# Opening of a two-block transformer kernel: the turns of the input moved around the first weight products

## The reference, cut to what matters

```python
c_act = jax.nn.silu(c)
mod = (c_act @ ada_w[0] + ada_b[0])
shift, scale, gate = jnp.split(mod, 3, axis=-1)
h = rmsnorm(x, norm_g[0]) * (1.0 + scale) + shift
proj = h @ ret_w_in            # 2048 x 12288, float32
```

## Time and profile before

| | |
|---|---|
| median of three runs | 2283.14 us (2281.1 to 2284.38) |
| profiled execution, its own time | 2281.51 us |
| its span | 2279.8 us |
| TensorE busy | 2221.4 us, 97% |
| weight loads into TensorE busy | 1844.3 us, 81% |
| DVE busy | 1488.4 us, 65% |
| ACT busy | 1038.5 us, 46% |
| mean DMA rate | 220 GB/s |

### The profile page before, as it was taken

One profiled execution on the slowest core, in us unless ns is written; L12 is line 12 of the kernel. 1 busy time (PEld: TensorE's weight loads), 2 busy tenths in 40 slices (PEclk: granted clock), 3 DMA queues, 4 the chain that ended last, 5 costly groups with the idle time before them and its releaser, 6 DMA issues.

```text
span 2279.8 us, 27033 instructions
## 1 busy us (share of the span) xinstructions
PE 2221.4 (97%) x10412; PEld 1844.3 (81%) x10412; DVE 1488.4 (65%) x1903; ACT 1038.5 (46%) x1353; POOL 98.9 (4%) x81
## 2 busy tenths in 40 slices
PE   5999999999999999999989999999999999999999
PEld 4878788878887788988868788877888888888887
DVE  7898778778877878556665555655555554555554
ACT  4544354444444445545454455444444344344442
POOL 0000000000000000000020200000100000000000
PEclk8999999999999999999989999999999999999999
DMA  9988577877896779545435554564666666666664
GB/s 349 379 330 291 170 269 270 308 263 286 297 312 214 293 252 330 184 132 174 167 128 205 154 175 142 168 194 152 189 185 186 194 186 192 193 185 193 187 188 143
DMA packets 139795, 501.92 MB, mean 220 GB/s; under 512 B 15633, under 2 KB 16145, under 8 KB 139153
## 3 DMA queue, kind: packets, MB, share of 16 engines
q1 hardware_dynamic: 139376, 499.99, 66.3%
q10 hardware_dynamic: 290, 0.21, 0.0%
HBM read 498.04 MB, written 2.10 MB: 219 GB/s over the span
## 4 chain that ended last, share of the span: by engine, by line
PE 88%; DVE 5%; DMA 3%; ACT 2%; issue 2%; POOL 1%; SPq 0%; DVEq 0%; ACTq 0%; POOLq 0%
PE ps L996 71%; PE ps L1007 7%; PE ps L1068 2%; PE ps L1021 2%; DMA raw<-in_ret_in 1%; PE ps L1060 1%; DVE wlo L1549 1%; DVE raw L1556 1%; DMA arena<-in_ret_in 1%; ACT whi L1241 1%; PE ps L1159 0%; POOL arena L1951 0%; DVE alo L1549 0%; PE ps L1136 0%; PE ps L1137 0%
## 5 line engine op out<-in xcount | busy, mean ns | idle before, releaser
L1549 DVE TENSOR_TENSOR wlo<-raw,whi 128x1024 fp32r<-128x1024 f32 (+1 forms) x711 | 864.4, 1221 | 585.4 <-ACT whi L1241 582.4
L1241 ACT ACTIVATE whi<-raw 128x1024 fp32r<-128x1024 f32 (+1 forms) x711 | 739.5, 1044 | 807.2 <-PE ps L996 651.9
L996 PE MATMUL ps<-whi,ahi 128*128 128x512 f32 x2482 | 788.0, 397 | 7.0 <-ACT whi L1241 4.0
L996 PE MATMUL ps<-wlo,ahi 128*128 128x512 f32 x2482 | 771.1, 390 | 4.8 <-DVE wlo L1549 4.7
L996 PE MATMUL ps<-whi,alo 128*128 128x512 f32 x2482 | 771.1, 391 | 0.0
L996 PEld LDWEIGHTS ps<-wlo,ahi 128*128 128x128 f32 x2482 | 466.1, 188 | 106.3 <-DVE wlo L1549 7.7
L996 PEld LDWEIGHTS ps<-whi,alo 128*128 128x128 f32 x2482 | 466.7, 188 | 98.4
L996 PEld LDWEIGHTS ps<-whi,ahi 128*128 128x128 f32 x2482 | 456.6, 189 | 99.6 <-ACT whi L1241 4.1
L1556 DVE SCALAR_TENSOR_TENSOR raw<-raw,arena 128x1024 f32<-128x1024 f32 x184 | 223.9, 1219 | 0.2
L1007 PE MATMUL ps<-whi,ahi 128*128 128x512 f32 x254 | 99.6, 392 | 0.0
L1007 PE MATMUL ps<-wlo,ahi 128*128 128x512 f32 x254 | 98.9, 389 | 0.0
(11 more groups left out here) (207 smaller groups left out, 1371.8 us busy)
## 6 DMA issues: line engine op xcount, KB each, us to landing
raw<-in_mlp SPq DMA_DIRECT2D x256, 512.0 KB, 4.2
raw<-in_ret_in SPq DMA_DIRECT2D x188, 512.0 KB, 5.0
raw<-in_ada_t SPq DMA_DIRECT2D x184, 512.0 KB, 5.0
raw<-in_in SPq DMA_DIRECT2D x80, 512.0 KB, 4.3
raw<-in_ret_out SPq DMA_DIRECT2D x64, 512.0 KB, 4.9
raw<-in_mla_in SPq DMA_DIRECT2D x48, 512.0 KB, 4.6
raw<-in_mla_out SPq DMA_DIRECT2D x32, 512.0 KB, 3.7
raw<-in_out SPq DMA_DIRECT2D x32, 512.0 KB, 4.1
```

The source lines that it names most:

```text
L996: mm = e.matmul(acc_[:, :], (ahi, alo, ahi)[m][:, slot, kb, tb * P:(tb + 1) * P], parts[m][:, chunk(n)], start=first and m == 0, stop=False)
L1241: e.activation(high(i)[:, 0:ncol], raw_of(n)[:, 0:ncol], ACT.Copy).then_inc(*s_hi.up(i))
L1549: e.tensor_tensor(low(i)[:, 0:ncol], raw_of(n)[:, 0:ncol], high(i)[:, 0:ncol].bitcast(F32), ALU.subtract).then_inc(*s_lo.up(i))
```

## The change

Five edits, all in the opening:

1. `pump(0, 3)` becomes `pump(0, 1)`: only load 0 and its adt stand before `norm_diag` in the list, where three did.
2. The DVE operation that makes the mean of h0 moves from `norm_diag` into `opening`, right behind the sums.
3. w0 is taken without a call of `pump`, so loads 6 to 23, their adt, mods and the splits of w2 to w7 no longer stand before block w0 but are queued by `next_block` for w1, together with loads 24 to 26 and the split of w8.
4. Behind block w0 come the turns of pairs 2 to 5 alone, in four banks that are free by then; the xn_out of each stands before those splits now.
5. The turns of pairs 6 and 7 become side jobs behind phase 0's side-by-side part: they run after blocks w8 and w9.

It follows that mod_first of kb 1 stands behind block w1 (and behind the split of w8), where it stood before block w1.

```diff
-    pump(0, 3)
+    pump(0, 1)
     do("norm_diag", "h0")
     pump(0, 6)
     turn_first(0)
...
-                w = next_block()
+                if kb == 0 and name == names[0]:
+                    w = at["used"]
+                    at["used"] += 1
+                else:
+                    w = next_block()
                 if i < len(kbs) - 1:
                     do("block", 0, ("h0", kb), w, 1024, got[name], begin)
-                    if kbs[0] == 0 and i == 0 and name == names[0]:
-                        for k2 in range(2, 8):
+                    if kb == 0 and name == names[0]:
+                        for k2 in range(2, 6):
                             turn_first(k2)
...
         if ph == 0:
+            side += [lambda k2=k2: turn_first(k2) for k2 in (6, 7)]
             do("later_in")
...
                 e.tensor_reduce(stat[:, 8:10], stat[:, 0:4].rearrange("p (t c) -> p t c", t=2), AX_X, ALU.add).then_inc(*s_vec.up(("sums", "h0")))
+                w.wait_ge(*s_vec.on(("sums", "h0")))
+                mean("h0", 0)
...
+            def mean(src, o):
+                e.tensor_scalar(stat[:, o + 10:o + 12], stat[:, o + 8:o + 10], 1.0 / D, EPS, ALU.mult, ALU.add).then_inc(*s_vec.up(("mean", src)))
+
             def norm_diag(src):
                 o = SUMS[src]
                 if src != "h0":
                     mean_square(src, o)
-                w.wait_ge(*s_vec.on(("sums", src)))
-                e.tensor_scalar(stat[:, o + 10:o + 12], stat[:, o + 8:o + 10], 1.0 / D, EPS, ALU.mult, ALU.add).then_inc(*s_vec.up(("mean", src)))
+                    w.wait_ge(*s_vec.on(("sums", src)))
+                    mean(src, o)
                 w.wait_ge(*s_pool.on(("rstd", src)))
```

## The result

The changed kernel takes 2288.16 us (median of nine runs, 2286.08 to 2289.53) against 2281.93 (nine runs, 2281.1 to 2284.38) before. The medians lie 6.2 us apart, the means 5.3; the ratio, which agrees with the means, is 1.0023 with a 95% interval of 1.0013 to 1.0034. The forecast was 2286.8, which is +3.7 us on the 2283.14 of the first three runs, and the range 2281.4 to 2289.4. The profiled span is 2286.4 us.

The account below looks back on a forecast made before the run. TensorE, busy 97% of the span, was taken as the bound, setting the pace from w2. 0.65 + 1.0 + 1.9 + 1.87 - 1.74 = +3.7 us on 2283.14 gave 2286.8 us, range 2281.4 to 2289.4.

Parts of the forecast that it names:

- likeliest case: Opening: w2 0.65 + L later, slow clock there, two turns added, wait at w32 gone: +3.7 us, 2286.8; chance 0.52.
- persistent wait: Rival at w32: later restart of loads carries through and the 1.74 us come back: +5.4, 2288.6; chance 0.12.
- upper clock bound: At w2: highest cost taken for TensorE's slow stretch after the long wait, 2.2 us against 1.9 forecast.
- first rival: At w0: block wholly slow, L = 2.0 instead of 1.0, w2 stretch at its 2.2: +5.0, 2288.1; chance 0.22.
- clock at w2: At w2: TensorE idles before it and meets it at 1.2 GHz, costing 1.9 us, bounds 1.5 and 2.2.
- L: At w0: cost of running at low clock after a gap behind the first turns; taken as 1.0 us, upper bound 1.9 to 2.2.
- The early turns: Opening: turns of pairs 0 and 1 start about 3.3 us earlier, near 13.1 instead of 16.42.
- The chain on DVE: From w2's rest to w7's: copies ahead of w2's split delay DVE, w7's rest ends 46.3 + L, w2 starts 0.65 + L later.
- The two turns: After w8 and w9: turns of pairs 6 and 7 move into TensorE's gapless part, costing 1.87 us.
- What is given back: At w32: TensorE arrives 1.87 us later than the loads do, so a wait of 1.74 us goes.
- two faster cases: At w2: delay hidden, start 47.8, -1.6 us, chance 0.08; or w2 5.35 early, -5.2 us, 2277.9, chance 0.06.
- hidden delay: On DVE: copies of pairs 2 to 5 cost splits nothing, w2 starts at 47.8; best end -1.6, 2281.5; chance 0.08.

Follow-up runs that it names:

- first and second experiments: First: changed kernel, mean and diagonals behind three adt again, ratio 1.0017. Second: kernel before with only the mean and diagonals moved early, ratio 1.0000.
- four blocks ahead: Staged kernel with its list running only four weight blocks ahead of the products up to w31, mean and diagonals behind three adt: ratio 0.9972, median 2275.70 us.
- third experiment: Changed kernel with splits of w2 and w3 queued before block w0, ahead of the four copies, mod_first of kb 1 behind w1: ratio 1.0004.
- filled wait: Changed kernel with 84 more matmuls in front of block w1, adding nothing to the output: ratio 1.0016.
- six turns: Changed kernel with the turns of pairs 6 and 7 also behind w0, their copies ahead of the split of w2: ratio 1.0025.
- two splits first: Same run as the third experiment: splits of w2 and w3 ahead of the four copies in the changed kernel, ratio 1.0004.
- late mean: Mean and diagonals behind three adt again (edits 1 and 2 undone); in the changed kernel ratio 1.0017, also combined with other runs.
- staged order: Changed kernel, list to w3's split before w0, w5's before w1, w7's before w2: ratio 1.0001; with mean and diagonals behind three adt 0.9994.

## Why the prediction was right, and where it was off

**Direction and size.** Forecast +3.7 us as the likeliest, measured +5.3 by the means and within the range. The forecast's own narrower range, up to 2288.1, was just missed by the median, 2288.16. Of the chances, "the same" within 0.2% had 0.62 and "slower" 0.32; the ratio says 0.23% slower, with an interval (0.13 to 0.34%) that holds both. By the prediction's own signs its likeliest case did not come: it called itself wrong if w2 started after 53, and w2 started at 53.25; w7's rest was to end by 48.3 and ended at 48.73. The upper edge of the range, 2289.4, does not follow from its terms either: the persistent wait with the upper clock bound gives 2283.14 + 5.4 + 0.3 = 2288.8. The case that came in kind was the first rival, w0 wholly slow, at +5.0. That its number lies so near the 5.4 of the rows is part luck: it had the clock at w2 0.45 too high, and left out 0.5 at w0 and 0.5 at w8's load.

**L, the clock at w0.** This is the term that was mis-sized: the sum has L = 1.0, the middle between two bounds, of which it said that neither is shown. The rows give 2.53, above the upper bound of 2.2. Of that 2.33 is twelve matmuls of which nearly all ran at half pace, 0.2 the later start of w0. The first and second experiments show that the early mean did this and that it costs only where the copies hold DVE; w0 was slow in all eight profiles with the early mean and in one of five with the late. What in it did so stays open: the turns began earlier and a gap of 3.1 us lay behind them, but four blocks ahead had a slow w0 behind a gap of 0.55. The Trainium skill, "TensorE: Matmul & The Clock Gate", section "HAM oscillation — how this bites in real kernels", describes such a pattern, a short piece of matmuls, a gap and the next piece at the low clock. The trace agrees in kind, since the twelve matmuls after the gap ran at 1.2 GHz (0.85 us a pair); the 4.8 us behind the gap of 0.55 are not told by it.

**The early turns.** The prediction had them at 13.1; they began at 14.04, since POOL's operation between the mean and the diagonals took 1.62 us and not 0.72. The gap was 3.1 us instead of 3.8.

**The chain on DVE.** Right, and shown by the third experiment: with L = 2.5 the prediction gives w7's rest at 48.8 and load 24 at 42.5; the rows have 48.73 and 42.47. Missing was 0.5 us: I had w8's load in time, at 49.0, and it landed at 50.55, 6.6 us after its issue at 43.98 behind two others, not 3.6 plus 1.3 each. From 44.5 to 50.5 the DMA moved 336 GB/s, where the prediction had 405. w2 came 3.70 late: 0.65 + 2.53 + 0.5.

**The clock at w2.** 1.9 us forecast, 1.75 measured, and shown by the filled wait.

**The two turns.** 1.87 forecast, 1.80 measured.

**What is given back.** 1.74 forecast; 3.70 + 1.75 + 1.80 - 5.38 leaves 1.87. The size is right, the reason only in part. The prediction let the loads move with w2 and put just the two turns between them and TensorE. In the rows TensorE reaches w8 5.46 us later, but the last split before w32's banks ran only 3.63 later (134.71 against 131.08), and DVE's wait for mod_first of kb 4 and 5, the tie that the prediction names, ended only 3.38 later (73.97 against 70.59). ACT's copies of finished banks, behind which it stands, came 3.4 later (70.25 against 66.83): before, they had themselves stood behind splits that waited for loads. The 1.8 us by which the loads moved less take the wait away with or without the turns, as reckoned at the six turns. In the two splits first the loads moved by 0.46 (131.54), and there the turns do carry it: w32 at 133.52 found banks whose copies began at 132.51.

**The other rivals.** The persistent wait and the two faster cases did not come. The third experiment built the hidden delay on purpose, and its shift of +0.4 is near the -1.6 that I gave as its best end plus the 1.75 of clock that I had left out there.

## What to carry to other kernels

On an engine that works strictly in order, what counts is not that a copy is early but what stands behind it and in front of it: a copy that must wait for TensorE delays the splits behind it (here 5 us), and a copy behind a split that waits for a far load delays TensorE (here 16, 1.5 and 10.7 us). Look for that pattern before moving work between engines, and limit how far loads are queued ahead where banks must be freed: here, with the late mean in both, that took the ratio of the staged order from 0.9994 to 0.9972. Work done earlier in front of a wait that stays can also be paid for in clock: 2.3 us at w0 behind the early turns, 1.75 at w2 behind the long wait. And before a term is put at the middle of two bounds, ask what either end would change; here L alone decided between +2.7 and +4.7.

## What the runs showed of the hardware that was not expected

The granted clock in the profile reads 1.00 in the first 30 us of the changed kernel, also while matmuls run at half pace (0.85 us a pair at 21 us, as under 0.50 at 53 us). There only the pace of the matmuls tells the level.

The rows show when the clock rose, not why. With the early mean w0 was slow in all eight profiles: 4.2 to 5.3 us from its start to the next turn. With the late mean it took 2.9 us in four of five profiles, and 4.8 in the fifth (four ahead), behind the same turns (16.37) and the same gap of 0.55 us. So the late mean does not keep w0 fast in every execution; it is 2 us more or less.

POOL's power operation took 1.62 or 1.63 us in all eight profiles with the early mean and 0.72 or 0.73 in the five with the late one; why was not looked into.
